# Halves of the output weights: stored in DRAM from block 0's projection and brought back for blocks 1 to 3, in place of raw loads and splits there

## What is computed

```
h    = rms_norm(x)
q, k, v, p = split(h @ w_in)                      # w_in 1024 x 1280
a    = sliding_window_attention(rms_norm(q), rms_norm(k), v, sinks)
m    = pooled means of p over 2, 4, 8, 16 rows, a linear map per group, a scale
x    = x + concat([a, m]) @ w_out                 # w_out 1024 x 1024
h2   = rms_norm(x)
out  = x + (silu(gate) * val) @ w_down            # gate, val: causal conv(3) of h2 @ w_up
```

## Time and profile before

| | us |
|---|---|
| median of 3 runs | 1767.29 (1766.17 to 1767.68) |
| the profiled execution | 1765.85 |
| its span, first to last instruction | 1764.1 |
| TensorE busy | 1748.3 (99%) |
| VectorE busy | 1340.5 (76%) |
| ScalarE busy | 822.2 (47%) |
| GpSimd busy | 302.0 (17%) |

### The profile page before, as it was taken

How to read it: one execution, slowest core, us unless ns; L and a number is a source line. 1 busy time by engine, 2 the same in 40 slices (tenths; PEclk the granted TensorE clock), 3 DMA queues, 4 the chain that set the end, 5 groups by cost and what they waited for, 6 DMA issues and landing times.

```text
span 1764.1 us, 23493 instructions
## 1 busy us (share of the span) xinstructions
PE 1748.3 (99%) x8454; PEld 1454.6 (82%) x8454; DVE 1340.5 (76%) x1773; ACT 822.2 (47%) x1448; POOL 302.0 (17%) x296
## 2 busy tenths in 40 slices
PE   8999999999999999999999999999999999999999
PEld 7787888888888888888888888888888888888887
DVE  4656856566789888889888878878877778865874
ACT  4565645535665444444454444444444433333321
POOL 2353312434110000000000000000004023220210
PEclk9999999999999999999999999999999999999999
DMA  8867688577747433332375232232237998976883
GB/s 325 282 226 281 237 323 297 206 286 263 252 154 259 136 95 120 132 95 72 132 279 174 84 96 72 84 91 77 79 95 242 345 354 316 306 254 222 293 287 131
DMA packets 224245, 355.30 MB, mean 201 GB/s; under 512 B 14650, under 2 KB 107010, under 8 KB 223106
## 3 DMA queue, kind: packets, MB, share of 16 engines
q1 hardware_dynamic: 204702, 301.31, 50.5%
q10 hardware_dynamic: 19427, 52.49, 7.6%
HBM read 273.00 MB, written 80.74 MB: 201 GB/s over the span
## 4 chain that ended last, share of the span: by engine, by line
PE 92%; DVE 3%; DMA 1%; ACT 1%; POOL 1%; issue 1%; SPq 0%; ACTq 0%; DVEq 0%
PE ps L1037 30%; PE ps L1039 29%; PE ps L1038 29%; DVE sums L1959 1%; PE ps L1214 1%; PE ps L1337 1%; POOL ss_q L2507 1%; PE ps L1238 1%; PE ps L1225 1%; DMA wP_d<-wp_kept 0%; DVE w_lo L1899 0%; PE ps L1109 0%; DMA raw<-in_w_in_dram 0%; DMA raw<-in_w_out_dram 0%; PE ps L1201 0%
## 5 line engine op out<-in xcount | busy, mean ns | idle before, releaser
L1037 PE MATMUL ps<-va_hi,wv 128*128 128x512 f32 x1232 | 479.4, 389 | 0.0
L1039 PE MATMUL ps<-va_hi,wv 128*128 128x512 f32 x1232 | 479.3, 389 | 0.0
L1038 PE MATMUL ps<-va_lo,wv 128*128 128x512 f32 x1232 | 479.3, 389 | 0.0
L1039 PEld LDWEIGHTS ps<-va_hi,wv 128*128 128x128 f32 x1232 | 231.3, 188 | 48.0
L1037 PEld LDWEIGHTS ps<-va_hi,wv 128*128 128x128 f32 x1232 | 231.3, 188 | 47.9
L1038 PEld LDWEIGHTS ps<-va_lo,wv 128*128 128x128 f32 x1232 | 231.3, 188 | 47.8
L1037 PE MATMUL ps<-dt_hi,ds_hi 128*128 128x512 f32 x616 | 239.6, 389 | 0.0
L1038 PE MATMUL ps<-dt_lo,ds_hi 128*128 128x512 f32 x616 | 239.6, 389 | 0.0
L1039 PE MATMUL ps<-dt_hi,ds_lo 128*128 128x512 f32 x616 | 239.6, 389 | 0.0
L2311 DVE SCALAR_TENSOR_TENSOR cb<-ub,cst,cb 128x1024 f32<-128x1024 f32 x176 | 217.8, 1279 | 8.3 <-ACT cb L1736 8.3
L1736 ACT ACTIVATE cb<-ub,cst 128x1024 f32<-128x1024 f32 x88 | 109.2, 1244 | 158.2 <-DVE ub L2360 94.5
(11 more groups left out here) (223 smaller groups left out, 2894.0 us busy)
## 6 DMA issues: line engine op xcount, KB each, us to landing
dg<-gT_d SPq DMA_DIRECT2D x264, 256.0 KB, 5.4
rw<-in_w_up_dram SPq DMA_DIRECT2D x84, 512.0 KB, 5.2
dw<-in_w_down_dram SPq DMA_DIRECT2D x132, 256.0 KB, 5.5
gT_d<-cb ACTq DMA_DIRECT2D x44, 512.0 KB, 2.6
w_hi<-wA_d SPq DMA_DIRECT2D x30, 512.0 KB, 4.2
w_lo<-wA_d SPq DMA_DIRECT2D x30, 512.0 KB, 6.2
n<-in_x_dram SPq DMA_DIRECT2D x16, 512.0 KB, 8.6
raw<-in_w_out_dram SPq DMA_DIRECT2D x16, 512.0 KB, 5.0
```

Source lines behind the costliest of these rows:

```text
L1037: pe.matmul(out_ap, l_hi, r_hi, start=first, stop=False, skip_group_check=True)
L1038: pe.matmul(out_ap, l_hi, r_lo, start=False, stop=False, skip_group_check=True)
L1039: return pe.matmul(out_ap, l_lo, r_hi, start=False, stop=last, skip_group_check=True)
```

## The change

Block 0's `o` units now count as kept: their halves are stored to wA_d after the split (eight units, two stores of 512 KB each), and the six `w` units of blocks 1 and 2 and the eight `o` units of block 3 are brought from there (`first_unit` finds the block 0 unit that holds the same weights). Twenty raw loads with their splits on ScalarE and VectorE become forty loads of 512 KB. The list is changed around it: `r_load` and `to_sum(1, 0)` go behind the queries; `to_hi` and `to_lo` of piece 0 go behind the first two `o` units; `n2sq(0)` and `av(1, 0)`, `av(1, 1)` go ahead of piece 3's sums, `n2sc(0)` ahead of `win(2, 1)`, and piece 3's store to behind `kv(2, 1)`, with the wait for it moved to the first `tb`. The score matmuls of block 0's tile 3 run inside `pin(1, 3)`, after its second of eight row tiles. In `w` the additions come ahead of the splits.

```diff
@@ attention_order
             units("kv", a, (1,))
+            if a == 2:
+                units("to_store", 1, (3,))
             units("kve", a, ())
@@
         units("q", a, (1,))
-        if a == 1:
-            units("r_load", a, ())
@@
             units("bias", a, ())
-            units("to_sum", a, (0,))
@@
         if a == 1:
+            units("r_load", a, ())
             units("to_load", a, (0,))
+            units("o", a - 1, (0, 0), (0, 1))
+            units("to_sum", a, (0,))
+            units("kt", a, ())
             units("to_hi", a, (0,))
-            units("o", a - 1, (0, 0), (0, 1))
             units("to_lo", a, (0,))
-            units("kt", a, ())
             units("o", a - 1, (0, 2))
             units("to_load", a, (1,), (2,))
@@
             units("win", a + 1, (0,))
+            units("av", a, (0,), (1,))
+            units("n2sq", a - 1, ())
             if a == 1:
                 units("to_sum", a, (3,))
-            units("av", a, (0,), (1,))
-            if a == 1:
                 units("to_hi", a, (3,))
-            units("n2sq", a - 1, ())
             units("pin", a + 1, (1,))
             if a == 1:
                 units("to_load", a, (3,))
+            units("n2sc", a - 1, ())
+            units("win", a + 1, (1,))
+            if a == 1:
                 units("to_lo", a, (3,))
-            units("win", a + 1, (1,))
-            units("n2sc", a - 1, ())
@@
-            if a == 1:
-                units("to_store", a, (3,))
@@ tables
-    if _s[1] == 0 or _s[0] in ("o", "w"):
+    if _s[1] == 0:
         SPLIT_NO[_n] = len(SPLIT_NO)
-KEPT_UNITS = [n for n in SPLIT_NO if UNITS[n][0] not in ("wp", "o", "w")]
+KEPT_UNITS = [n for n in SPLIT_NO if UNITS[n][0] != "wp"]
@@ first_unit
+    if name == "w":
+        i, k = args
+        return UNIT["o", 0, int(i == 6), k + 2 * (i == 1)]
@@ SyncE, w and tb
-                if (b, i, k) == (1, 0, 0):
-                    sp.wait_ge(S["fold_out"], T_STORED)
...
+                if (b, u) == (1, 0):
+                    sp.wait_ge(S["fold_out"], T_STORED)
@@ TensorE, pin and s
+                    if (a, g, i) == (1, 3, 2):
+                        scores(0, 3)
...
             def s(a, t):
+                if (a, t) != (0, 3):
+                    scores(a, t)
+
+            def scores(a, t):
@@ VectorE, w
-                if i == 6:
-                    split(n + LEAD)
                 if k == 1:
                     added(b, i, 0)
                     added(b, i, 1)
+                if i == 6:
+                    split(n + LEAD)
@@ VectorE, q
+                    if t == 3 and a - 1 in SEVEN:
+                        split(UNIT["w", a - 1, 1, 1])
                     if t:
                         scaled(a, t - 1)
-                if a - 1 in SEVEN:
-                    split(UNIT["w", a - 1, 1, 1])
                 scaled(a, NT - 1)
```

## The result

The changed kernel takes 1769.86 us (median of 10 runs, 1767.99 to 1774.02), the kernel before beside it 1765.62 us (10 runs, 1763.63 to 1767.68). The ratio is 1.0027, with a 95% interval of 1.0017 to 1.0036: slower by 0.3%. The forecast was 1765.1, with no change the likeliest; the median lies 0.4 us above the end of its range (1769.5). That range was laid around the median of three runs of the kernel before, 1767.29; against the ten runs beside it the forecast was -2.2 us and the result is +4.2. The profiled execution took 1768.06 us (span 1766.3), 2.2 us more than that of before.

What follows compares the result with a forecast made beforehand. TensorE's waits in the first 500 us (6.0 us) and the lower clock behind one bound what could be won. +2.1 - 4.3 - 0.6 + 0.6 = -2.2 us, so 1765.1 against the median 1767.29; range 1761.5 to 1769.5.

Steps and rivals of the forecast that it cites:

- the price of a store in SyncE's queue: Store of `o(0, 0, 0)`'s halves ahead of `o(0, 0, 3)`'s raw weights: net 1.0 to 2.1 us later, taken as 1.6.
- the gain around 230 us: Squares and scaling moved ahead: waits of 2.1 and 0.5 us and 1.7 us of lower clock go, 4.3 us gained.
- the sums of `tb`: Brought sums behind SyncE's wait for a ring slot; TensorE wants them only later, so costed at nothing.
- The signs that the prediction named: Profile after: waits near 168 and 238 gone, new 2 to 4 us wait before `o(0, 1, 0)`, `pin(2, 0)` at 214 to 215.5.
- the w_lo wait: TensorE's 1.9 us wait before `o(0, 0, 2)` at 168.13, foretold to go as `to_sum(0)` moves away.
- The stretch to `pin(2, 0)`: 140 to 215 us: late VectorE chain gives the early gain back; `pin(2, 0)` about 2.1 us later, bounds +1.4 and +2.9.
- the gap in SyncE's queue that I credited: Gap behind the load at 153.61, said to take up 1 to 1.5 us of the store ahead of the raw weights.
- the 2.4 us gained before: TensorE starts `o(0, 0, 2)` at some 165.7 in place of 168.13, as the split comes about 2.3 us earlier.
- rival (3): Clock falls after the idle 3.2 us before `o(0, 1, 0)`; 1765.6 to 1767.3, chance 0.15 shared with another rival.
- late pairs of `w(b, 1, 0)`: Blocks 1 and 2: brought pairs wait for ring slots, stall 0 to 1.3 us each, taken as 0.3 each, 0.6 lost.
- The splits: Twenty removed ScalarE and VectorE splits in blocks 1, 2 and 3; only 0.5 and 0.1 us of waits go, 0.6 us gained.
- Rival (2): Block 1's added stores crawl and delay raw weights of `o(0, 0, 3)`; a landing at 173 gives +3.8, 1771; chance 0.11.

Runs made afterwards that it cites:

- e1: Changed kernel with its new order only: the twenty units come raw and are split, no output-weight halves stored; 1760.35 us.
- e8: e1 with to_sum(0) ahead of q(1,2), r_load behind the first two raw o units, o(0,0,2)'s low half in the query sums' last pause; 1757.49 us.
- e9: Changed kernel without storing o(0,1,2) and o(0,1,3); block 3's two units with the same weights come raw; 1767.44 us.
- e3: Changed kernel with to_sum(0) moved between o(0,0,0) and o(0,0,1) in the list; 1768.95 us.
- e5: e1 with the halves of block 0's eight units stored to DRAM where nobody reads them; 1768.15 us.
- e7: Changed kernel with the edits of e3, e4 and e9 together; 1759.69 us.
- e12: e1 with only the last two pairs, o(0,1,2) and o(0,1,3), stored where nobody reads them; 1765.21 us.
- e10: Kernel before with the new order around 230 us, and piece 3's store moved behind kv(2,1); 1761.18 us.
- e6: Kernel before with only the new order around 230 us, piece 3's store not moved; 1768.46 us.
- e4: Changed kernel with the loads of pairs w(b,6,0) and w(b,6,1) moved behind tb(4) and tb(6) in blocks 1 and 2; 1768.57 us.
- e11: e8 with six of the eight units stored and brought, and e4's order; 1758.68 us.

## Why the prediction was wrong

The profiled execution was forecast to gain 2.2 us and lost 2.2. Of these 4.4 us TensorE's timeline puts 1.2 before `pin(2, 0)` (+3.3 for +2.1), 1.2 between it and `w(1, 0, 0)` (-3.1 for -4.3), and 2.0 behind (+2.0 for -0.6 + 0.6). Three steps failed: the price of a store in SyncE's queue was too low, the gain around 230 us was counted in full beside it, and the sums of `tb` were put at nothing. The signs that the prediction named came out, but for 0.8 us of the w_lo wait that stayed and for `pin(2, 0)`, 0.4 us later than said; it had named none for the sums of `tb` and for block 2's pairs. That the median is only 0.4 us outside the range owes something to luck, since the range started from a median of before that was 1.7 us above that of the ten runs.

**The stretch to `pin(2, 0)`: mechanism right, size short.** The raw weights of `o(0, 0, 3)` landed at 167.9 (forecast 167.0, outer bound 167.9), the low half, `to_sum(0)`, `to_hi(0)`, `to_lo(0)` and the additions followed each other as worked out, the additions at 183.90 (183.1) and TensorE at 184.73 (183.8). The store's price was 3.1 us (e1 to the changed kernel) and not 1.6, since the gap in SyncE's queue that I credited was not there: the load ahead of the store went out only at 154.14 (before 153.61), and the loads of pieces 1 and 2 right behind the store. Of the 2.4 us gained before only 1.5 came; `r_load`, put ahead of the raw loads, made the first of these late (split at 151.79, before 149.23, in e8 with `r_load` behind them 146.81), a queue that I passed over. From `o(0, 1, 0)` to `pin(2, 0)` 1.6 us more were lost. The clock fell there, which is rival (3), but most of this would have been lost without it: in e9, after the same wait but at full clock, the stretch is 30.6 us long, against 29.6 before and 31.2 in the changed kernel, and it is 30.6 in e1, e3, e5, e7 and e12 too. So 1.0 us is the late VectorE, forecast as 1.3, and some 0.6 the clock, which rival (3) had at 0.5. Sum +3.3 for +2.1.

**Around 230: a condition left out.** I wrote that the squares come up to 6.1 us earlier and "the scaling perhaps 5". The squares did come earlier; the scaling overwrites the rows and waits for their stores, and what is in the DMA queues at that time was left out of the step. As a change of order the term was right (e10: 4.5 us), and its hidden condition, the moved store of piece 3, was in the change (e6). With all halves stored, the profiled execution lost 1.2 us of it to the late pair of `pin(2, 2)`, and it had the rest only because TensorE arrived late: it reached `t2(0, 0)` at 239.71, 3.1 us after the scaling had begun. On time, it would have waited, as in e12 (3.7 us). Even late it was luck: in e4's execution of the same steps TensorE waits 3.5 us there. So with these stores the +3.3 and the -4.3 were not to be added, the one was the condition of the other; without the last two of them both come out side by side (e9: +3.1 to `pin(2, 0)`, -4.5 from there to `w(1, 0, 0)`).

**The pairs and `tb`: the largest part.** The 0.6 us for late pairs of `w(b, 1, 0)` did not occur. What I costed at nothing behind them did: sums of `tb` waited for behind two pairs that nobody needs for 30 us. `w(1, 0, 0)` to `w(2, 0, 0)` lost 1.5 us by it, and block 2 about as much, before the gains named next; e4 takes it away.

**The splits.** 0.6 us were put on the twenty removed splits (22 instead of 42 on ScalarE remain). In e1, where all are still there, the same places gain 0.4 us (`w(2, 1, 1)`) and 0.8 (`o(3, 0, 0)`): it was the change of order, most likely the additions put ahead of the splits, and not the removal.

**Rival (2)** had the right cause and even the ring ("brought pairs for the ring, which multiplies it"), but I priced it by one landing alone, that of `o(0, 0, 3)`, and set the end of its range by it. The stores that cost most were the last two (e12: 4.9 of 7.8 us), where no row of that landing could show it.

**What stays open.** The medians differ by 4.2 us, the profiled executions by 2.2. The changed kernel scatters over 6.0 us, e1 over 2.1. The clock has a part in it: of the ten executions of the changed kernel the five with a mean granted clock of 0.999 or 1.000 took 1767.99 to 1769.34 us, the five at 0.998 took 1770.38 to 1774.02, and 0.001 of the span is 1.8 us. It does not explain the whole, since at the same 0.999 the changed kernel took 1768.06 to 1769.34 and the kernel before, beside e1, 1764.30 to 1766.30. Row stores that land later in one execution than in another, as between the changed kernel's and e4's, are one cause that is shown; how often it happens in the others was not traced.

## What to carry to other kernels

Storing something "beside" other work is not free because the DMA engines have room on average: ask which slot is held until the store has landed, what is loaded into that slot, and which other queue's transfers then fall into the same stretch. A gain behind a loss is only counted in full if it stands when the loss is gone; test the parts apart, here the order was worth 5 us, and the halves took all of it and 4 more. Fixes that give 1 or 2 us each can be worth 10 together when each is given back to a wait that another removes. One profiled execution is one draw: where two transfers race, a wait that it does not show can stand in the next.

## What the runs showed of the hardware

The lower clock does not follow a wait by its length. In the profiled executions, of twelve waits of TensorE between 2.1 and 4.2 us from 150 to 250 us, six were followed by a stretch at the lower level. The same wait before `o(0, 1, 0)`, 3.4 us in e9 and 3.2 in the changed kernel (clock 0.62 there), left e9 at full clock:

```profile
185.10:188.60 3.50, 3.50 (x15) 2.89 (x16) 2.97 (x5) 2.15 (x2) 0.00 (x0) 1.00 0.98 391
```

The runs of the kernels whose profile has no such wait (e1, e7, e8, e10) spread over 1.7 to 2.6 us, those of the others, but for e11, over 3.2 to 9.7; they were run more often (10 or 11 times for 5 to 7), which is part of the difference. It fits an extra that a long wait costs in some executions only, and so do the clocks of the single executions (e7, e8 and e11 at 1.000 in all five each, the changed kernel at 0.998 in five of ten), but it was not tested by itself.
